# Feed-forwards of a two-block network on one core: one level of Strassen's identity on 256-column blocks

## The reference

```
def swiglu(x, w_gate, w_up, w_down):
    return (jax.nn.silu(x @ w_gate) * (x @ w_up)) @ w_down
x = layer_norm(alpha * x + 0.5 * swiglu(x, w_gate, w_up, w_down), ln_g, ln_b)
```

## Time and profile before

| | |
|---|---|
| median of 3 runs | 2386.46 us (2380.72 to 2388.42) |
| the profiled execution | 2380.86 us |
| its span | 2378.9 us |
| PE, PE weight loads, DVE, ACT busy | 82%, 52%, 15%, 9% of the span |
| HBM | 253 GB/s over the span |
| mean granted TensorE clock | 0.91 |

### The profile page before, as it was taken

The page is one execution under the profiler, slowest core; times in us unless marked ns, Lnnn a source line. Parts: engine busy times, 40 slices in busy tenths (PEclk is TensorE's granted clock), DMA queues, the critical chain, the costliest instruction groups (busy, mean ns, idle before and its releaser), DMA issues.

```text
span 2378.9 us, 20900 instructions
## 1 busy us (share of the span) xinstructions
PE 1944.8 (82%) x9324; PEld 1227.4 (52%) x9324; DVE 363.2 (15%) x785; ACT 220.1 (9%) x423; POOL 17.3 (1%) x41
## 2 busy tenths in 40 slices
PE   6987566665666665665999999999999999989997
PEld 5755222222222222221677777777677767857775
DVE  1213111111011111100100032200120015240002
ACT  4231000000000000000100010100010002110000
POOL 1100000000000000000000000000000000000000
PEclk9999878888888888777999999999999999989999
DMA  9246999999999999999644442544454444334440
GB/s 282 72 177 270 427 427 428 428 427 428 428 427 428 428 427 429 427 428 408 204 159 155 145 142 90 189 146 159 142 165 149 146 154 129 107 106 159 152 149 18
DMA packets 181777, 604.28 MB, mean 254 GB/s; under 512 B 17773, under 2 KB 135975, under 8 KB 157111
## 3 DMA queue, kind: packets, MB, share of 16 engines
q1 hardware_dynamic: 176064, 595.51, 65.0%
q10 hardware_dynamic: 5623, 7.42, 1.1%
HBM read 601.86 MB, written 1.05 MB: 253 GB/s over the span
## 4 chain that ended last, share of the span: by engine, by line
PE 66%; DMA 28%; DVE 2%; ACT 1%; SPq 1%; issue 1%; ACTq 0%; DVEq 0%
PE banks L1211 26%; PE banks L1225 10%; DMA e_W<-in_expert_w_gate 10%; DMA e_W<-in_expert_w_down 10%; DMA e_W<-in_expert_w_up 8%; PE banks L869 6%; PE banks L1256 5%; PE banks L191 3%; PE banks L877 3%; PE banks L1300 2%; PE banks L1244 2%; PE banks L1376 2%; SPq L849 1%; PE banks L386 1%; PE banks L392 1%
## 5 line engine op out<-in xcount | busy, mean ns | idle before, releaser
L1211 PE MATMUL banks<-x_xT,x_ring 128*128 128x256 f32 x2816 | 621.6, 382 | 3.5 <-DVE x_xT L1591 2.9
L1211 PEld LDWEIGHTS banks<-x_xT,x_ring 128*128 128x128 f32 x2816 | 539.7, 192 | 94.5 <-issue 21.9
L869 PE MATMUL banks<-e_W,e_xT 128*32 128x512 f32 x2048 | 288.2, 726 | 190.2 <-DMA e_W<-in_expert_w_up 104.5
L869 PEld LDWEIGHTS banks<-e_W,e_xT 128*32 128x32 f32 x2048 | 79.1, 130 | 387.0 <-issue 385.8
L877 PE MATMUL banks<-e_W,e_hT 128*32 128x512 f32 x1024 | 147.5, 741 | 142.8 <-DMA e_W<-in_expert_w_down 142.8
L1225 PE MATMUL banks<-x_ring,x_hT 128*128 128x512 f32 x576 | 253.1, 592 | 0.0
L1225 PEld LDWEIGHTS banks<-x_ring,x_hT 128*128 128x128 f32 x576 | 109.4, 190 | 122.4 <-issue 120.5
L877 PEld LDWEIGHTS banks<-e_W,e_hT 128*32 128x32 f32 x1024 | 40.5, 133 | 238.3 <-issue 238.3
L1628 DVE TENSOR_TENSOR x_hT<-x_act,banks 128x256 f32<-128x256 f32 x88 | 37.1, 422 | 812.8 <-ACT x_act L1490 812.8
L1256 PE MATMUL banks<-x_xT,x_ring 128*128 128x256 f32 x544 | 122.1, 386 | 1.6 <-issue 1.6
L1256 PEld LDWEIGHTS banks<-x_xT,x_ring 128*128 128x128 f32 x544 | 104.8, 194 | 17.6 <-issue 3.1
(11 more groups left out here) (405 smaller groups left out, 1031.9 us busy)
## 6 DMA issues: line engine op xcount, KB each, us to landing
e_W<-in_expert_w_gate SPq DMA_DIRECT2D x64, 2048.0 KB, 20.9
e_W<-in_expert_w_up SPq DMA_DIRECT2D x64, 2048.0 KB, 20.6
e_W<-in_expert_w_down SPq DMA_DIRECT2D x64, 2048.0 KB, 21.2
x_ring<-in_ffn_w_gate SPq DMA_DIRECT2D x44, 1024.0 KB, 5.3
x_ring<-in_ffn_w_up SPq DMA_DIRECT2D x44, 1024.0 KB, 5.4
x_ring<-in_ffn_w_down SPq DMA_DIRECT2D x44, 1024.0 KB, 4.9
x_ring<-in_w_in_mlstm SPq DMA_DIRECT2D x13, 1024.0 KB, 5.2
x_ring<-in_w_in_conv SPq DMA_DIRECT2D x10, 1024.0 KB, 5.1
```

Source lines behind the costliest of these rows:

```text
L869: i = pe.matmul(ps[SLOT * j:SLOT * (j + 1), b, :], E.xT[:, x, k, SLOT * j:SLOT * (j + 1)], E.W[:, slot0 + j, k * DE:(k + 1) * DE], start=( ...
L1211: mm = pe.matmul(ps[:, 2 * b + f2, which * S:(which + 1) * S], w8(i)[:, k, f2 * P:(f2 + 1) * P], N.xT[:, k, :], start=(k == 0), stop=(k == ...
```

## The change

The product of a block's weights and the tokens is cut into 2x2: the 1024 model columns into two halves, the 256 hidden columns into two, the tokens into two. Strassen's identity (in Winograd's form) then has seven products of half blocks where there were eight, with sums of blocks as operands, and sums of products as results. For down, the halves are those of tokens, hidden columns and output columns.

- The four sums of weights that a chunk needs are made on DVE (weight_sums: four tensor_tensor over 512 columns) into one of four slots; those of the tokens (token_sums) once in a feed-forward, and those of the hidden block (hidden_sums: four over 128 columns) on DVE too.
- On PE a block is plain(c), products 1 and 2, which need no sums, and mixed(c), products 3, 5, 7, 6, 4. Each product is 2 weights x 4 k-tiles of matmuls with 128x128 weights and 128 moving columns. Blocks alternate between banks 0 to 3 and 4 to 7. plain(0) needs only the first token half, and turn(j, 1) stands behind it.
- ACT copies product 1 to SBUF (keep), DVE combines the seven (post, seven operations of 256 columns), ACT takes Silu of 512 columns, DVE multiplies (hidden, 512 columns).
- All down products of a feed-forward come after all its gate and up products. Seven matmuls of 512 columns to a block accumulate into seven banks, and the chunks are loaded in that order. DVE combines the seven once, at the end (merged), in place of sums in norm.
- rows(j) moves from the end of norm behind block 0 of the next feed-forward, or to the head of the mixer on DVE; constants move from the start into the mixers; load_rows moves behind block 2 on ACT; ACT's spread of the first token half moves ahead of the second root. ffn(2)'s first two weight sums are made at the end of ffn(1).
- Buffers are laid out anew: the sums and the whole hT take the upper half of what the expert weights had.

The diff, cut to its core (lines taken out are those of the functions printed above; indented less than in the file):

```
+BANK_AT = [0, 0, 6, 9, 15, 21, 24]
+GU = {1: (0, 0), 2: (1, 0), 4: (1, 256), 6: (2, 0), 7: (2, 256), 5: (3, 0), 3: (3, 256)}
+DB = {1: 0, 2: 1, 6: 2, 5: 3, 3: 4, 7: 5, 4: 6}
...
+            load(at + 2 * c, w8(at + 2 * c), wg[n][:, :, c * FC:(c + 1) * FC])
+            load(at + 2 * c + 1, w8(at + 2 * c + 1), wu[n][:, :, c * FC:(c + 1) * FC])
+        for c in range(NFC):
+            i = at + 2 * NFC + c
+            load(i, w2(i), wd[n][:, 2 * c:2 * c + 2, :])
...
+        def product(c, p):
+            bank, lo = GU[p]
+            bank += 4 if c % 2 == 0 else 0
+            for which in range(2):
+                i = at + 2 * c + which
+                w, m = w8(i), N.sums[:, sum_slot(n, 2 * c + which), :, :].rearrange("p j (k f) -> p j k f", k=4)
+                for k in range(4):
+                    a, b = {1: (w[:, k, 0:P], N.xT[:, k, t0]), 2: (w[:, 4 + k, 0:P], N.xT[:, 4 + k, t0]),
+                            3: (m[:, 3, k, :], N.xT[:, 4 + k, t1]), 4: (w[:, 4 + k, P:FC], N.xs[:, 3, k, :]),
+                            5: (m[:, 0, k, :], N.xs[:, 0, k, :]), 6: (m[:, 1, k, :], N.xs[:, 1, k, :]),
+                            7: (m[:, 2, k, :], N.xs[:, 2, k, :])}[p]
+                    mm = pe.matmul(ps[:, bank, lo + which * P:lo + (which + 1) * P], a, b, start=(k == 0), stop=(k == 3))
+                if p == 1 and which:
+                    mm.then_inc(s["lone"], 1)
+                if p == 6:
+                    mm.then_inc(s["used"], 1)
+                if p == 4:
+                    mm.then_inc(s["spent"], 1)
+        def plain(c):
+            wait_chunk(pe, at + 2 * c)
+            wait_chunk(pe, at + 2 * c + 1)
             if c >= 2:
...
+                pe.wait_ge(s["post"], NFC * n + c - 1)
+            product(c, 1)
+            product(c, 2)
+        def mixed(c):
+            pe.wait_ge(s["sum"], FPOS * n + 2 * c + 2)
+            for p in (3, 5, 7, 6, 4):
+                product(c, p)
+        def down(c, p):
+            i, q = at + 2 * NFC + c, c % 4
+            w, m = w2(i), N.sums[:, sum_slot(n, 2 * NFC + c), :, :]
+            a, b = {1: (N.hT[:, c, 0, :], w[:, 0, 0:512]), 2: (N.hT[:, c, 2, :], w[:, 1, 0:512]),
+                    3: (N.hs[:, q, 3, :], w[:, 1, 512:D]), 4: (N.hT[:, c, 3, :], m[:, 3, :]),
+                    5: (N.hs[:, q, 0, :], m[:, 0, :]), 6: (N.hs[:, q, 1, :], m[:, 1, :]), 7: (N.hs[:, q, 2, :], m[:, 2, :])}[p]
+            mm = pe.matmul(ps[:, DB[p], :], a, b, start=(c == 0), stop=(c == NFC - 1))
+            if p == 4:
+                mm.then_inc(s["spent"], 1)
+            elif c == NFC - 1:
+                mm.then_inc(s["bank"], 1)
+        def wait_down(c):
+            wait_chunk(pe, at + 2 * NFC + c)
+            pe.wait_ge(s["sum"], FPOS * n + 2 * NFC + c + 1)
+            pe.wait_ge(s["hsum"], NFC * n + c + 1)
+        turn(j, 0)
+        pe.wait_ge(s["xt_v"], TT * j + 1)
+        pe.wait_ge(s["xt_a"], TT * j + 1)
+        plain(0)
+        turn(j, 1)
+        plain(1)
+        pe.wait_ge(s["tx"], n + 1)
+        mixed(0)
+        mixed(1)
         for c in range(2, NFC):
+            plain(c)
+            mixed(c)
+        pe.wait_ge(s["post"], NFC * n + NFC - 1)
+        for c in range(2):
+            wait_down(c)
+            for p in (1, 2, 6, 5):
+                down(c, p)
+        pe.wait_ge(s["post"], NFC * n + NFC)
+        for c in range(2):
+            for p in (3, 7, 4):
+                down(c, p)
+        for c in range(2, NFC - 2):
+            wait_down(c)
+            for p in (1, 2, 6, 5, 3, 7, 4):
+                down(c, p)
+        wait_down(NFC - 2)
+        wait_down(NFC - 1)
+        for p in (1, 2, 6, 5, 3, 7, 4):
+            down(NFC - 2, p)
+            down(NFC - 1, p)
...
     front.tensor(pe)
     moe.tensor(pe)
     ffn(0, 0)
+    for t in range(TT):
+        turn(1, t)
     conv()
     ffn(1, 2)
     ffn(2, 3)
+    for t in range(TT):
+        turn(4, t)
     lstm()
     ffn(3, 5)
 @block.scalar
...
-            if t == 1 and j < 6:
+            if t == 0 and j < 6:
                 spread(j, 0)
         if j < 6:
             spread(j, 1)
...
+        def keep(c):
+            base = 4 if c % 2 == 0 else 0
+            a.wait_ge(s["lone"], NFC * n + c + 1)
+            a.activation(N.p1[:, c % 2, :, :], ps[:, base, 0:FC].rearrange("p (w t) -> p w t", w=2), ACT.Copy).then_inc(s["kept"], 1)
+        keep(0)
+        keep(1)
         for c in range(NFC):
+            a.wait_ge(s["post"], NFC * n + c + 1)
+            if c >= 2:
+                a.wait_ge(s["hid"], NFC * n + c - 1)
+            a.activation(N.act[:, c % 2, :, :], N.cb[:, c % 2, :, 0, :], ACT.Silu).then_inc(s["act"], 1)
+            if c < NFC - 2:
+                keep(c + 2)
+            if c == 2:
+                load_rows(j + 1)
+        a.wait_ge(s["bank"], BANK_AT[j + 1] + 1)
+        a.activation(N.pd[:, :], ps[:, DB[1], :], ACT.Copy).then_inc(s["kept"], 1)
...
+    def merged(n, j, scale, last):
+        add = lambda t, m, x: K.vc.mark(v.scalar_tensor_tensor(out=h[:, t, m * 512:(m + 1) * 512], in0=x, scalar=scale,
+                                                               in1=h[:, t, m * 512:(m + 1) * 512], op0=ALU.mult, op1=ALU.add))
+        after = lambda n: v.wait_ge(K.vc.sem, n)
+        got = lambda n: v.wait_ge(s["bank"], BANK_AT[j] + n)
+        prod = lambda p: ps[:, DB[p], :]
+        stats = lambda t, m: v.bn_stats(N.stats[:, t, m, :], h[:, t, m * 512:(m + 1) * 512])
+        both = lambda o, x, y: K.vc.mark(v.tensor_tensor(N.ud[:, o, :], x, y, ALU.add))
+        v.wait_ge(s["kept"], (NFC + 1) * (n + 1))
+        x = add(0, 0, N.pd[:, :])
+        got(3)
+        u2 = both(0, N.pd[:, :], prod(6))
+        after(x)
+        x = add(0, 0, prod(2))
+        got(4)
+        after(u2)
+        u4 = both(1, N.ud[:, 0, :], prod(5))
+        after(x)
+        stats(0, 0)
+        after(u4)
+        x = add(0, 1, N.ud[:, 1, :])
+        got(5)
+        after(x)
+        c(add_last(0, 1, prod(3), scale))
+        c(stats(0, 1))
+        v.bn_aggr(N.mv[:, 0, :], N.stats[:, 0, :, :]).then_inc(s["mv"], 1)
+        got(6)
+        u3 = both(2, N.ud[:, 0, :], prod(7))
+        after(u3)
+        x = add(1, 1, N.ud[:, 2, :])
+        y = add(1, 0, N.ud[:, 2, :])
+        scaled(j, 0)
+        after(x)
+        x = add(1, 1, prod(5))
         if j < 6:
             spread(j, 0)
+        after(x)
+        stats(1, 1)
+        v.wait_ge(s["spent"], last)
+        after(y)
+        c(add_last(1, 0, prod(4), scale))
+        c(stats(1, 0))
+        v.bn_aggr(N.mv[:, 1, :], N.stats[:, 1, :, :]).then_inc(s["mv"], 1)
         scaled(j, 1)
         if j < 6:
             spread(j, 1)
...
+    def weight_sums(n, x):
+        i, before = AT_FFN[n] + x, sum_before(n, x)
+        if before:
+            m, y = before
+            if y < 2 * NFC:
+                v.wait_ge(s["used"], 2 * NFC * m + y + 1)
+            else:
+                v.wait_ge(s["spent"], AT_FFN[m] + y + 1)
+        wait_chunk(v, i)
+        o = N.sums[:, sum_slot(n, x), :, :]
+        if x < 2 * NFC:
+            o, w = o.rearrange("p j (k f) -> p j k f", k=4), w8(i)
+            a11, a12, a21, a22 = w[:, 0:4, 0:P], w[:, 4:8, 0:P], w[:, 0:4, P:FC], w[:, 4:8, P:FC]
+            first = K.vc.mark(v.tensor_tensor(o[:, 0], a21, a22, ALU.add))
+            v.tensor_tensor(o[:, 2], a11, a21, ALU.subtract)
+            v.wait_ge(K.vc.sem, first)
+            c(v.tensor_tensor(o[:, 1], o[:, 0], a11, ALU.subtract))
+            v.tensor_tensor(o[:, 3], a12, o[:, 1], ALU.subtract).then_inc(s["sum"], 1)
+        else:
+            w = w2(i)
+            b11, b12, b21, b22 = w[:, 0, 0:512], w[:, 0, 512:D], w[:, 1, 0:512], w[:, 1, 512:D]
+            first = K.vc.mark(v.tensor_tensor(o[:, 0], b12, b11, ALU.subtract))
+            v.tensor_tensor(o[:, 2], b22, b12, ALU.subtract)
+            v.wait_ge(K.vc.sem, first)
+            c(v.tensor_tensor(o[:, 1], b22, o[:, 0], ALU.subtract))
+            v.tensor_tensor(o[:, 3], b21, o[:, 1], ALU.subtract).then_inc(s["sum"], 1)
+    def token_sums(n, j):
+        v.wait_ge(s["xt_v"], TT * (j + 1))
+        v.wait_ge(s["xt_a"], TT * (j + 1))
+        b11, b12, b21, b22 = N.xT[:, 0:4, 0:P], N.xT[:, 0:4, P:S], N.xT[:, 4:8, 0:P], N.xT[:, 4:8, P:S]
+        first = K.vc.mark(v.tensor_tensor(N.xs[:, 0], b12, b11, ALU.subtract))
+        v.tensor_tensor(N.xs[:, 2], b22, b12, ALU.subtract)
+        v.wait_ge(K.vc.sem, first)
+        c(v.tensor_tensor(N.xs[:, 1], b22, N.xs[:, 0], ALU.subtract))
+        v.tensor_tensor(N.xs[:, 3], b21, N.xs[:, 1], ALU.subtract).then_inc(s["tx"], 1)
+    def ffn(n, j, again=False):
         at = AT_FFN[n]
+        def post(cc):
+            v.wait_ge(s["spent"], at + 2 * cc + 2)
+            if n or cc:
+                v.wait_ge(s["post"], NFC * n + cc)
+            if cc >= 2:
+                v.wait_ge(s["act"], NFC * n + cc - 1)
+                v.wait_ge(s["hid"], NFC * n + cc - 1)
+            base = 4 if cc % 2 == 0 else 0
```

(126 more changed lines are left out.)

78 lines of the change are left out of this document (23 added, 55 removed).

## The result

The changed kernel takes 2316.03 us (median of 4 runs, 2315.02 to 2317.05) against 2383.59 us (median of 4, 2379.1 to 2388.42) for the kernel before: a ratio of 0.9716, 95% interval 0.9694 to 0.9739. That is 2.8% faster. The forecast was 2319 us in a range of 2300 to 2346. The span of the profiled execution fell from 2378.9 to 2313.0 us, by 65.9; the sum had said 66.

What follows compares the result with a forecast made beforehand. The prediction took TensorE's instructions, plus a seam at either end, to bound each feed-forward. Gains of 56 us in gate/up and 38 in down, less 28 in seams, gave 66 off 2380.86: 2315, a median of 2319 us, range 2300 to 2346.

Steps and rivals of the forecast that it cites:

- the sum: Whole kernel: 94 us gained in gate/up and down matmuls, less 28 us lost around the feed-forwards, leaves 66 us.
- The pace of short matmuls: Gate/up: each 128-column instruction takes 112 ns, so a block takes 12.54 us against 13.81, 56 us gained in all.
- Rival (a): Gate/up: short matmuls don't hold 112 ns over a thousand in a row; at 123 ns no gain, 2376 us; chance 0.07.
- (c): Gate/up: weight loading is the bound, every load occupying the load path for 192 ns, 2714 us; chance 0.04.
- Down: Down matmuls: seven products of 512 columns in place of eight, 6.01 us a block against 6.87, 38 us gained.
- DVE's cover: Gate/up blocks: DVE's new work of 8.3 us lies under PE's 12.54 us, covered by 4 us.
- Rival (b): Gate/up blocks: DVE becomes the bound, a block takes 13.5 us, 44 us more, 2363 us; chance 0.05.
- The starts: Before mixed(0) of each feed-forward: changes of +7.4, +6, -0.8 and +6 us for feed-forwards 0 to 3.
- The 2 us for the clock: Starts of feed-forwards 0, 1 and 3: the clock falls after PE's wait, 2 us added each (0 to 4).
- The ends: After the last down matmul: +3.5 us each at feed-forwards 0 and 2, +2.8 to the output at feed-forward 3.
- the seams: Starts and ends of the four feed-forwards together: 28 us lost.

## Why the prediction was right

**The pace of short matmuls** was the term that carried most: 112 ns taken, 111.9 measured over 1168 in a row. The gather and the 64-column attention had given it from 32 at a time. That it is a floor which the moving columns don't set was shown with 64 and 96 columns; that the load sets it, as the prediction read from L1281, fits these and the 54.6 ns of weights half as wide. Rival (a) (the pace does not hold) and (c) (loads one after another, 192 ns) are out. With (c) goes the rule of the Trainium skill, TensorE: Matmul & The Clock Gate, Part 3, that a load overlaps with matmuls in flight only where its row group differs: by it an instruction would take the prediction's estimate of 214 ns at full clock. The trace disagrees: loads and matmuls of the whole array are both busy for 118 of 118 us, with one pair every 112 ns.

**Down**, 6.01 us for a block: 14 x 429.3 ns, shown by the eighth product.

**DVE's cover**: 8.3 us and 4 to spare were forecast, 8.1 and 4.43 measured. Rival (b) is out, and the two runs with more sums place its threshold: 2.9 us more is free and 5.8 is not.

**The starts.** For feed-forward 1, mixed(0) was forecast 17.0 us after the last matmul of the mixer; it started at 1496.48 - 1479.24 = 17.2. The 2 us for the clock were 133.0 - 130.7 = 2.3, and 2.9 and 2.7 in feed-forwards 0 and 3. Counted from the end of the stage before to the last down matmul, and less the 23.5 us gained in the matmuls, the starts cost +8.8, +4.5, -0.6 and +6.0 for feed-forwards 0 to 3; the forecast was +7.4, +6, -0.8 and +6. Feed-forward 1 was cheaper than forecast because plain(0) ran at full clock (3.84 us for 32 instructions), which it did not in feed-forwards 0, 2 and 3 (6.38, 5.37, 5.47). Feed-forward 0 was dearer by those 6.38 us, for which 5.8 had been written, and by the 2.9 for the clock.

In one step of the starts the size was off: mixed(0) of feed-forward 2 was put at 12.2 us after the last down matmul, and came at 1709.99 - 1695.5 = 14.5. The step left out that plain(0) meets the lower clock there (5.37 us in place of 3.6), as the first gate and up matmuls had before (0.57 in the earlier trace rows), and it had 0.9 us for the spread behind turn(j, 1), which on ACT takes 1.52. Since the kernel before paid for the lower clock too, the difference between the two kernels came out nearly right.

**The ends.** The chain at the end of feed-forward 0, whose last matmul ends at 1294.29 + 66.1 = 1360.4:

```profile
1358.92 0.56 DVE x_ud L1670
1359.51 1.29 DVE c_h L1664 x2
1360.91 1.00 DVE c_h L1629 x2
1361.92 0.60 DVE c_h L1664
1362.75 1.04 DVE x_xT L1637 x3
1363.79 0.60 DVE n_stats L1669
1364.39 0.60 DVE c_h L1712
1365.02 0.70 DVE n_stats L1669
...
1366.52 0.56 DVE c_h L1629
```

u3 starts 1.5 us before that end (forecast 1.6), the scaling of half 1 is 6.1 behind it (6.3), and all of the steps between are DVE's, as written down. conv started 10.3 us after the end in place of 7.3, lstm 10.3 in place of 6.5: +3.0 and +3.9 for the 3.5 forecast. The output came +1.7 later, not +2.8. With the starts the seams sum to 27.3 us; 28 was forecast.

That sums of single terms this small hold to a microsecond in total is partly luck: +1.4 and -1.5 at two starts cancel. The first block, which the sum does not have, ended 1.7 us later in this profile than in the one before, so that the 65.9 us between the two spans lie closer to the 66 of the sum than the method can promise.
